# A two-block model on one core: the statistics, banks and order of the mLSTM mixer rearranged

## The chip, the core and the metric

The kernel runs on one core of a Trainium2 chip. A core has five engines that work side by side, each with its own queue of instructions: TensorE (PE, matmuls into the eight PSUM banks), VectorE (DVE), ScalarE (ACT, which loads a table for each family of functions), GpSimd (POOL) and SyncE (SP, which issues transfers here). They meet by semaphores alone. The metric is the device time of one execution in microseconds, the median of three runs.

## The reference, cut to what matters

The model is a hybrid block (a convolution branch and an mLSTM branch, then a mixture of experts) and a second block with a delta-rule mixer, attention and two feed-forward layers. Only the first block's mixer is touched:

```python
z = h @ w_in                       # 512 tokens, 1024 -> 5128 features
u = causal_dwconv(glu_a * sigmoid(glu_b), conv_dw_w, conv_dw_b)     # 31 taps
u = silu(layernorm(u, conv_ln_g, conv_ln_b))                        # over 512 channels
y_a = u @ w_conv_out                                                # 512 -> 1024
qk = silu(causal_dwconv(concat([q, k]), qk_conv_w, qk_conv_b))      # 4 taps
hm = mlstm_chunkwise(q, k, v, i_g, f_g)                             # 4 heads of 128
hm = (hm - mean) * rsqrt(var + eps) * m_norm_g * sigmoid(o)         # per head
y_b = hm @ w_m_out                                                  # 512 -> 1024
merged = sigmoid(g_a) * y_a + sigmoid(g_b) * y_b
x = x + gate * (merged @ w_out)
```

The kernel computes mLSTM in one piece per head: with running decay sums, weights exp(...) of every earlier token on every later one times the scores q.k give P; the numerator is v'P, the denominator the column sum of P, and h = numerator / max(|denominator|, exp(-m)).

## The kernel before

Features lie on the partitions, the 512 tokens along the free side. A is a big SBUF buffer of 59 rows of 512 columns; A[:, 8 to 11] hold the four heads' results, A[:, 40 to 43] the conv branch, A[:, 44 to 51] q and k, A[:, 16 to 19] v, A[:, 24 to 39] the two sets of gates, A[:, 52 to 55] a head's weights. PS is PSUM, eight banks of 128x512.

Projections are done in 40 tiles (p = 4g + j, ten groups of four), each of 24 matmuls: every product is made of three (high x high, high x low, low x high), for which ScalarE writes a weight piece's high part and VectorE its low part. Group g uses banks 4(g % 2) to 4(g % 2) + 3, and ScalarE copies every tile out, the last groups through a sigmoid. Behind them stands, in TensorE's order: the transposes of v for tokens (L607), the sums over channels for the conv norm's mean (L614) and variance (L618), four small transposes of gate values (L623), then the heads. ScalarE does Silu of q and k (L1203), the squares (L1207), the root by Ln and Exp (L1136, L1137) and Silu of the normed conv channels (L1212). Only then do the heads begin.

For each of four heads: TensorE spreads a row over the partitions (bank 4, L634), makes four score blocks in banks 0 to 3 (L640), and a second row (bank 5); VectorE copies the first row twice (L1733, L1734), ScalarE takes seven exponentials of it (L1237, L1240), VectorE multiplies scores and exponentials (L1759), TensorE makes numerators (bank 6, L650) and denominators (bank 7, L652), ScalarE takes the absolute value (L1242), VectorE the maximum, the reciprocal and the product (L1763 to L1765), which raises ml_h. TensorE waits for ml_h of a head before it starts the next head's numerators, and VectorE divides a head before it makes the next head's weights:

```python
for hd in range(MH):
    if hd:
        pe.wait_ge(S("ml_h"), hd)
    head_row(hd, 5, gr[7])
```

Between heads ScalarE and VectorE split one conv channel tile (L1244, L1767) and one out weight piece (L1220, L1741) into high and low parts. After head 3: means of all heads on TensorE (L659), differences (L1772), squares (L1248), sums (L662), Ln (L1251), Exp (L1254), and VectorE applies norm, gain and gate (L1775, L1776). TensorE waits for ml_std of all heads, then does 16 out tiles of 12 matmuls (q = 0 to 7 from conv_out, 8 to 15 from m_out), each multiplied by its gate on VectorE (L1786, L1792), summed in pairs (L1794), split (L1265, L1752), and eight w_out tiles of 24 matmuls, whose results are added to x (L1810). SyncE loads the second w_out unit when the last m_out tile is done, behind it x, and then the first experts' weights.

## Time and profile before

| | us |
|---|---|
| median of three runs (2561.7 to 2565.02) | 2563.48 |
| the profiled execution | 2564.16 |
| its span, first to last instruction | 2562.4 |
| TensorE busy in it | 2313.2 |
| VectorE busy | 1182.8 |
| ScalarE busy | 813.5 |
| mean granted TensorE clock, share of full | 0.942 |

Times in rows are microseconds from the span's start. The profile puts down what ended an engine's idle time, by semaphores; PE rows are pipelined, so starts tell more than lengths. The granted clock is 1.00 for 2.4 GHz and 0.50 for 1.2 GHz. Read a stage by what ends its idle times, not by the busy shares of the whole span.

### The profile page before, as it was taken

How to read it: one execution, taken by the hardware profiler on the slowest of the kernel's cores; microseconds unless marked ns; L12 is line 12 of the kernel's file. 1: busy time of each engine (PE TensorE's matmuls, PEld its weight loads, DVE VectorE, ACT ScalarE, POOL GpSimd, SP SyncE). 2: the span in 40 equal slices, each digit the busy share in tenths (PEclk: the TensorE clock that was granted, in tenths of full speed). 3: DMA queues.
4: the chain of work that ended last, by engine and by line, in shares of the span. 5: the costliest groups of instructions: out<-in, count | busy, mean ns of one | idle time of the engine just before them, and what ended most of it. 6: DMA issues, size and time to landing. Idle time of an engine off the chain costs nothing.

```text
span 2562.4 us, 29704 instructions
## 1 busy us (share of the span) xinstructions
PE 2313.2 (90%) x11748; PEld 1584.8 (62%) x11748; DVE 1182.8 (46%) x1716; ACT 813.5 (32%) x1251; POOL 119.6 (5%) x160
## 2 busy tenths in 40 slices
PE   6899878959999999957989498999999899999997
PEld 3688636623333333324768496888777787888775
DVE  3789345430000000025654743677843573677832
ACT  3222333321111111124455253323324283323322
POOL 0000000021111111100000200000000000000000
PEclk8999978979999999978989689999999999999999
DMA  8622200628999999830111001122222301222221
GB/s 356 226 79 92 92 0 33 277 91 332 375 378 399 386 389 385 359 137 34 66 66 66 1 34 66 66 98 98 99 99 99 132 1 66 81 90 95 95 99 66
DMA packets 36406, 384.56 MB, mean 150 GB/s; under 512 B 10080, under 2 KB 10336, under 8 KB 13408
## 3 DMA queue, kind: packets, MB, share of 16 engines
q1 hardware_dynamic: 27520, 374.91, 37.5%
q0 software_dynamic: 8800, 8.45, 1.0%
q8 instruction: 60, 0.98, 0.2%
q14 instruction: 26, 0.21, 0.0%
HBM read 384.10 MB, written 16.83 MB: 156 GB/s over the span
## 4 chain that ended last, share of the span: by engine, by line
PE 53%; DVE 16%; ACT 5%; issue 3%; DMA 1%; DVEq 1%; POOL 0%; ACTq 0%; SPq 0%; POOLq 0%
PE PS L744 9%; PE PS L570 9%; PE PS L571 9%; PE PS L572 8%; PE PS L783 4%; PE PS L764 4%; DVE ring_r L1946 3%; PE PS L791 2%; DVE A L1694 2%; ACT w_hi_r L1318 2%; PE PS L533 2%; DVE A L2156 1%; DVE sq L2154 1%; DVE A L2157 1%; DVE hid_r L2169 1%
## 5 line engine op out<-in xcount | busy, mean ns | idle before, releaser
L571 PE MATMUL PS<-h_r,w_hi_r 128*128 128x512 f32 x1104 | 432.5, 392 | 0.0
L570 PE MATMUL PS<-h_hi_r,w_hi_r 128*128 128x512 f32 x1056 | 418.0, 396 | 10.8 <-ACT A L1345 7.5
L572 PE MATMUL PS<-h_hi_r,ring_r 128*128 128x512 f32 x1056 | 413.3, 391 | 0.0
L1946 DVE TENSOR_TENSOR ring_r<-ring,w_hi_r 128x1024 fp32r<-128x1024 f32 x196 | 238.6, 1223 | 362.7 <-ACT w_hi_r L1318 362.7
L1318 ACT ACTIVATE w_hi_r<-ring 128x1024 fp32r<-128x1024 f32 x196 | 202.6, 1051 | 329.0 <-PE PS L572 203.9
L570 PEld LDWEIGHTS PS<-h_hi_r,w_hi_r 128*128 128x128 f32 x1056 | 199.7, 189 | 62.3 <-issue 17.2
L571 PEld LDWEIGHTS PS<-h_r,w_hi_r 128*128 128x128 f32 x1104 | 209.2, 190 | 45.0 <-issue 1.9
L572 PEld LDWEIGHTS PS<-h_hi_r,ring_r 128*128 128x128 f32 x1056 | 199.6, 189 | 42.1
L1922 DVE TENSOR_TENSOR A<-A,PS 128x512 f32<-128x512 f32 x16 | 11.0, 687 | 396.4 <-PE PS L744 396.4
L744 PE MATMUL PS<-A 128*64 128x512 f32 x768 | 170.4, 600 | 0.1
L570 PE MATMUL PS<-x_r,top_r 128*128 128x512 f32 x320 | 128.2, 400 | 12.0 <-DVE ring_r L1605 12.0
L571 PE MATMUL PS<-hid_r,w_hi_r 128*128 128x512 f32 x352 | 138.5, 393 | 0.0
L571 PE MATMUL PS<-h_r,top_r 128*128 128x512 f32 (+1 forms) x328 | 130.7, 398 | 0.0
L572 PE MATMUL PS<-x_r,ring_r 128*128 128x512 f32 x320 | 126.6, 395 | 0.0
L744 PEld LDWEIGHTS PS<-A 128*64 128x64 f32 x768 | 54.9, 138 | 113.2 <-issue 113.0
L783 PE MATMUL PS<-A 128*64 128x512 f32 x256 | 113.3, 595 | 0.0
L783 PE MATMUL PS<-h,A 128*64 128x512 f32 x256 | 113.3, 595 | 0.0
L764 PE MATMUL PS<-A 128*32 128x512 f32 x768 | 113.1, 594 | 0.0
L1694 DVE SCALAR_TENSOR_TENSOR A<-A,vec 128x511 f32<-128x511 f32 (+9 forms) x144 | 106.1, 737 | 4.1
L1497 ACT ACTIVATE A<-A 128x512 f32<-128x512 f32 x44 | 27.8, 632 | 250.7 <-DVE A L2157 250.7
L1170 ACT ACTIVATE top_r<-ring 128x1024 fp32r<-128x1024 f32 x40 | 42.4, 1060 | 168.7 <-PE PS L572 168.7
L570 PE MATMUL PS<-top_r,w_hi_r 128*128 128x512 f32 x208 | 83.0, 399 | 10.9 <-DVE ring_r L1946 6.7
(448 smaller groups left out, 3762.6 us busy)
## 6 DMA issues: line engine op xcount, KB each, us to landing
A<-wexp SPq DMA_DIRECT2D x64, 2048.0 KB, 12.3
ring<-wall SPq DMA_DIRECT2D x63, 2048.0 KB, 8.1
ring<-wexp SPq DMA_DIRECT2D x16, 2048.0 KB, 18.1
h<-wexp SPq DMA_DIRECT2D x16, 2048.0 KB, 13.2
A<-wada SPq DMA_DIRECT2D x12, 2048.0 KB, 14.7
x<-xt_in SPq DMA_DIRECT2D x2, 2048.0 KB, 12.1
A<-y_assignments SPq DMA_DIRECT2D x4, 1024.0 KB, 7.9
h_tokens<-A SPq DMA_DIRECT2D x4, 512.0 KB, 2.8
```

Source lines behind the costliest of these rows:

```text
L533: mm(PS[:, bank, :], ones, sq[:, k % 2, :], start=k == 0, stop=k == KD - 1).then_inc(S("sq_used"), 1)
L570: mm(out, w[0], x_[0], start=first, stop=False)
L571: mm(out, w[0], x_[1], start=False, stop=False)
L572: return mm(out, w[1], x_[0], start=False, stop=last_)
L744: last = mm(PS[HALF * j:HALF * (j + 1), bank, :], x_main[:, k // 4, (k % 4) * P + HALF * j:(k % 4) * P + HALF * (j + 1)], w[j][:, k, :], s ...
L764: last = mm(PS[r:r + QUARTER, 5, :], x_rest[:, k * HALF + QUARTER * j:k * HALF + QUARTER * (j + 1)], w[j][:, k, :], start=k == 0, stop=k = ...
L783: last = mm(PS[HALF * j:HALF * (j + 1), 6 + half, :], hT_main[:, k * P + HALF * j:k * P + HALF * (j + 1)], moe_dn[j][:, 4 * half + k, :], ...
L791: last = mm(PS[r:r + QUARTER, 5, :], hT_rest[:, k * HALF + QUARTER * j:k * HALF + QUARTER * (j + 1)], moe_dn[j][:, 4 * half + k, :], start ...
L1170: a_(in_hi(p), ring[:, g % 2, :, j * P:(j + 1) * P], ACT.Copy).then_inc(S("w_hi"), 1)
L1318: a_(w_hi_r[:, :, j * P:(j + 1) * P], ring[:, slot, :, j * P:(j + 1) * P], ACT.Copy).then_inc(S("w_hi"), 1)
L1694: ins = stt(dst[:, s:T], src[:, 0:T - s], w(j), dst[:, s:T], ALU.mult, ALU.add)
L1946: tt(ring_r[:, slot, :, cols], ring[:, slot, :, cols], w_hi_r[:, :, cols].bitcast(F32), ALU.subtract).then_inc(S("w_lo"), 1)
```

## The change

TensorE's order: the transposes of v go behind tile 36 (into banks 0 to 3), the conv mean and the small transposes behind tile 37, the conv variance (bank 3 in place of 2) behind tile 38. ScalarE copies v out after tile 36, and does the Silu of q and k and the conv squares after tile 37. Scores take three banks (the fourth block of 128 columns shares bank 1 with the second), numerators two in turn (6 and 3). A head's second row is made after the next head's scores, and waits for the division before. VectorE makes the next head's weights first and divides then; the conv channels are normed behind head 0's weights, their Silu lies behind head 0's exponentials on ScalarE. Conv pieces and inputs are split in sets (one, two, one input; one, one, two pieces) over heads 0 to 2. Out tiles 0 and 1 are before the head means, 2 and 3 before the head variances, 4 to 7 behind them, each in a bank of its own with a wait on one gate product in place of four; m_out and w_out tiles likewise. VectorE does gate products and pieces between the steps of the head norm. The short convolutions come in the order of the heads. In the diff, blank lines and parts that repeat the old text in another place are left out.

```diff
@@ -334,6 +334,30 @@
...
+        def mix_bank(q):
+            return 4 + q % 4 if q // 4 in (2, 4) else q % 4
+        def num_bank(hd):
+            return 6 if hd % 2 == 0 else 3
+        def s_row4(hd):
+            return 3 * hd if hd else 1
+        def s_scores(hd):
+            return 3 * hd + 1 if hd else 2
+        def s_row5(hd):
+            return 3 * hd + 5 if hd + 1 < MH else 3 * MH
+        HEAD_INPUTS, HEAD_PIECES = ((0,), (1, 2), (3,), ()), ((0,), (1,), (2, 3), ())
+        HEAD_ORDER = [hd + part for hd in range(MH) for part in (0, MH)]
+        def score_place(s):
+            return PS[:, (0, 1, 2, 1)[s], 384 * (s == 3):384 * (s == 3) + T - s * P]
@@ -580,6 +604,36 @@
...
+            def v_rows():
+                pe.wait_ge(S("ev_act"), 36)
+                for t in range(NT):
+                    for hd in range(MH):
+                        last = nc.tensor.transpose(PS[:, t, hd * P:(hd + 1) * P], A[:, 16 + hd, t * P:(t + 1) * P], ident)
+                last.then_inc(S("gT_mm"), 1)
+            def conv_mean():
+                pe.wait_ge(S("ev_act"), 38)
...
+                for i in range(CT):
+                    last = mm(PS[:, 0, :], ones, A[:, 40 + i, :], start=i == 0, stop=i == CT - 1)
...
+            def conv_var():
+                for i in range(CT):
+                    pe.wait_ge(S("cl_sq"), i + 1)
+                    last = mm(PS[:, 3, :], ones, A[:, 4 + i, :], start=i == 0, stop=i == CT - 1)
+                last.then_inc(S("cl_mm"), 1)
+            def gate_columns():
...
+                    last = nc.tensor.transpose(PS[:, 2, 256 + 4 * t:260 + 4 * t], gr[5][:, t * P:(t + 1) * P], ident[0:4, 0:4])
+                last.then_inc(S("gT_mm"), 1)
@@ -600,100 +654,99 @@
...
+                    if p == 36:
+                        v_rows()
+                    if p == 37:
+                        conv_mean()
+                        gate_columns()
+                    if p == 38:
+                        conv_var()
+            pe.wait_ge(S("g_rows"), 2)
+            pe.wait_ge(S("em"), 1)
             pe.wait_ge(S("gT_ev"), 1)
-            pe.wait_ge(S("cl_ev"), 1)
-            pe.wait_ge(S("em"), 1)
...
                 return mm(PS[:, bank, :], ident[0:4, hd:hd + 1].broadcast_to([4, P]), src, start=True, stop=True)
             def head_scores(hd):
+                pe.wait_ge(S("ev_act"), 39)
                 head_row(hd, 4, gr[6]).then_inc(S("ml_s"), 1)
+                pe.wait_ge(S("qk"), 2 * hd + 2)
                 for s in range(NT):
-                    last = mm(PS[:, s, 0:T - s * P], A[:, 48 + hd, s * P:(s + 1) * P], A[:, 44 + hd, s * P:T], start=True, stop=True)
+                    last = mm(score_place(s), A[:, 48 + hd, s * P:(s + 1) * P], A[:, 44 + hd, s * P:T], start=True, stop=True)
                 last.then_inc(S("ml_s"), 1)
+            def head_end(hd):
+                if hd:
+                    pe.wait_ge(S("ml_h"), hd)
+                head_row(hd, 5, gr[7]).then_inc(S("ml_s"), 1)
             head_scores(0)
+            pe.wait_ge(S("ev_act"), 41)
...
             for hd in range(MH):
                 if hd:
-                    pe.wait_ge(S("ml_h"), hd)
-                head_row(hd, 5, gr[7])
+                    pe.wait_ge(S("ml_ad"), hd)
                 for s in range(NT):
                     pe.wait_ge(S("ml_p"), NT * hd + s + 1)
-                    mm(PS[:, 6, s * P:T], A[:, 16 + s, hd * P:(hd + 1) * P], A[:, 52 + s, s * P:T], start=s == 0,
...
                 last.then_inc(S("ml_n"), 1)
                 if hd + 1 < MH:
                     head_scores(hd + 1)
...
+                head_end(hd)
+            def head_means():
+                pe.wait_ge(S("ml_h"), MH)
+                for hd in range(MH):
+                    mm(PS[:, 4 + hd, :], ones, A[:, 8 + hd, :], start=True, stop=True).then_inc(S("ml_mu"), 1)
+            def head_vars():
+                for hd in range(MH):
+                    pe.wait_ge(S("ml_sq"), hd + 1)
+                    mm(PS[:, 4 + hd, :], ones, A[:, 12 + hd, :], start=True, stop=True).then_inc(S("ml_var"), 1)
+            def out_tile_of(q, u_hi, u_lo):
...
+                pe.wait_ge(S("w_lo"), PIECES_IN + q + 1)
...
+                    last = product(PS[:, mix_bank(q), :], (out_hi(q)[:, k, :], w_lo[:, k, :]), (u_hi(k), u_lo(k)), k == 0, k == CT - 1)
+                last.then_inc(S("mm"), 1)
+            pe.wait_ge(S("h_lo"), KD + CT)
+            for q in range(8):
+                if q == 2:
+                    head_means()
+                if q == 4:
+                    head_vars()
+                if q >= 4:
+                    pe.wait_ge(S("ev_dve"), q - 3)
+                out_tile_of(q, lambda k: h_r[:, k, :], lambda k: h_hi_r[:, 2 + k, :])
             pe.wait_ge(S("ml_std"), MH)
...
+            pe.wait_ge(S("h_lo"), 2 * KD)
+            for q in range(8, 16):
+                if q >= 12:
+                    pe.wait_ge(S("ev_dve"), q - 7)
+                out_tile_of(q, lambda k: hid_r[:, 16 + k, :], lambda k: hid_r[:, 8 + k, :])
...
+            norm(1, NORM_BANK[1])
@@ -1187,29 +1240,27 @@
...
+                    if p == 36:
+                        act.wait_ge(S("gT_mm"), 1)
+                        a_(A[:, 16:20, :], PS[:, 0:4, :], ACT.Copy).then_inc(S("ev_act"), 1)
+                    if p == 37:
+                        for n, m in enumerate(HEAD_ORDER):
+                            act.wait_ge(S("qk_cv"), n + 1)
+                            a_(A[:, 44 + m, :], A[:, 44 + m, :], ACT.Silu).then_inc(S("qk"), 1)
+                        for i in range(CT):
+                            act.wait_ge(S("cl_d"), i + 1)
+                            a_(A[:, 4 + i, :], A[:, 40 + i, :], ACT.Square).then_inc(S("cl_sq"), 1)
...
+            inv_sqrt(rstd[:], PS[:, 3, :], 1, 1.0 / DC).then_inc(S("cl_ev"), 1)
@@ -1238,25 +1289,36 @@
...
+                if hd == 0:
+                    for i in range(CT):
+                        act.wait_ge(S("cl_n"), i + 1)
+                        a_(A[:, 40 + i, :], A[:, 40 + i, :], ACT.Silu, bias=V("conv_ln_b", i)).then_inc(S("ya_in"), 1)
                 act.wait_ge(S("ml_n"), hd + 1)
+                if hd:
+                    act.wait_ge(S("ml_h"), hd)
                 a_(A[:, 2, :], PS[:, 7, :], ACT.Abs).then_inc(S("ml_ad"), 1)
-                act.wait_ge(S("ya_in"), hd + 1)
-                a_(h_r[:, hd, :], A[:, 40 + hd, :], ACT.Copy).then_inc(S("h_hi"), 1)
-                out_w_hi(hd)
+                for i in HEAD_INPUTS[hd]:
+                    act.wait_ge(S("ya_in"), i + 1)
+                    a_(h_r[:, i, :], A[:, 40 + i, :], ACT.Copy).then_inc(S("h_hi"), 1)
+                for q in HEAD_PIECES[hd]:
+                    out_w_hi(q)
+            out_w_hi(4)
             for hd in range(MH):
                 act.wait_ge(S("ml_d"), hd + 1)
                 a_(A[:, 12 + hd, :], A[:, 8 + hd, :], ACT.Square).then_inc(S("ml_sq"), 1)
+            for q in range(5, 8):
+                out_w_hi(q)
             for hd in range(MH):
                 act.wait_ge(S("ml_var"), hd + 1)
                 last = a_(A[:, 4 + hd, :], PS[:, 4 + hd, :], ACT.Ln, bias=eps[:, 1:2], scale=1.0 / P)
...
+            for hd in range(MH):
+                out_w_hi(8 + hd)
+                act.wait_ge(S("hm"), hd + 1)
+                a_(hid_r[:, 16 + hd, :], A[:, 8 + hd, :], ACT.Copy).then_inc(S("h_hi"), 1)
+            for q in range(12, 16):
@@ -1709,7 +1771,7 @@
...
-            for m in range(8):
+            for m in HEAD_ORDER:
@@ -1720,16 +1782,19 @@
...
+            cp(gT[:], PS[:, 2, 256:272].rearrange("p (a b) -> p a b", b=MH)).then_inc(S("gT_ev"), 1)
+            def conv_normed():
+                dve.wait_ge(S("cl_ev"), 1)
+                dve.wait_ge(S("cl_d"), CT)
+                for i in range(CT):
+                    stt(A[:, 40 + i, :], A[:, 40 + i, :], V("conv_ln_g", i), rstd[:], ALU.mult, ALU.mult).then_inc(S("cl_n"), 1)
@@ -1751,45 +1816,71 @@
...
-            head_rows(0)
-            for hd in range(MH):
-                dve.wait_ge(S("ml_s"), 2 * hd + 2)
+            def head_weights(hd):
+                dve.wait_ge(S("ml_s"), s_scores(hd))
...
-                    stt(A[:, 52 + s, s * P:T], PS[:, s, 0:T - s * P], float(P) ** -0.5, A[:, 52 + s, s * P:T], ALU.mult, ALU.mult).then_inc(S("ml_p"), 1)
+                    stt(A[:, 52 + s, s * P:T], score_place(s), float(P) ** -0.5, A[:, 52 + s, s * P:T], ALU.mult, ALU.mult).then_inc(S("ml_p"), 1)
+            def head_divided(hd):
+                dve.wait_ge(S("ml_ad"), hd + 1)
+                dve.wait_ge(S("ml_s"), s_row5(hd))
+                link(tt(A[:, 2, :], A[:, 2, :], PS[:, 5, :], ALU.max))
+                link(nc.vector.reciprocal(A[:, 3, :], A[:, 2, :]))
+                tt(A[:, 8 + hd, :], PS[:, num_bank(hd), :], A[:, 3, :], ALU.mult).then_inc(S("ml_h"), 1)
+            head_rows(0)
+            head_weights(0)
+            conv_normed()
+            for hd in range(MH):
                 if hd + 1 < MH:
                     head_rows(hd + 1)
-                dve.wait_ge(S("ml_ad"), hd + 1)
-                link(tt(A[:, 2, :], A[:, 2, :], PS[:, 5, :], ALU.max))
-                link(nc.vector.reciprocal(A[:, 3, :], A[:, 2, :]))
-                tt(A[:, 8 + hd, :], PS[:, 6, :], A[:, 3, :], ALU.mult).then_inc(S("ml_h"), 1)
-                dve.wait_ge(S("h_hi"), KD + hd + 1)
-                tt(h_hi_r[:, 2 + hd, :], A[:, 40 + hd, :], h_r[:, hd, :].bitcast(F32), ALU.subtract).then_inc(S("h_lo"), 1)
-                out_w_lo(hd)
+                    head_weights(hd + 1)
+                head_divided(hd)
+                for i in HEAD_INPUTS[hd]:
+                    dve.wait_ge(S("h_hi"), KD + i + 1)
+                    tt(h_hi_r[:, 2 + i, :], A[:, 40 + i, :], h_r[:, i, :].bitcast(F32), ALU.subtract).then_inc(S("h_lo"), 1)
+                for q in HEAD_PIECES[hd]:
+                    out_w_lo(q)
...
+                dve.wait_ge(S("mm"), out_tile(q))
...
+                tt(u, u, PS[:, mix_bank(q), :], ALU.mult).then_inc(S("ev_dve"), 1)
...
+                dve.wait_ge(S("ml_std"), hd + 1)
+                link(stt(A[:, 8 + hd, :], A[:, 8 + hd, :], V("m_norm_g", hd), A[:, 4 + hd, :], ALU.mult, ALU.mult))
...
+            gated(0)
+            out_w_lo(4)
+            gated(1)
...
-                stt(A[:, 8 + hd, :], PS[:, hd, :], -1.0 / P, A[:, 8 + hd, :], ALU.mult, ALU.add).then_inc(S("ml_d"), 1)
+                stt(A[:, 8 + hd, :], PS[:, 4 + hd, :], -1.0 / P, A[:, 8 + hd, :], ALU.mult, ALU.add).then_inc(S("ml_d"), 1)
+            for q in (2, 3):
+                out_w_lo(q + 3)
+                gated(q)
+            out_w_lo(7)
...
+                head_normed(hd)
+                gated(4 + hd)
+                out_w_lo(8 + hd)
             for hd in range(MH):
-                out_w_lo(4 + hd)
                 dve.wait_ge(S("h_hi"), KD + CT + hd + 1)
                 tt(hid_r[:, 8 + hd, :], A[:, 8 + hd, :], hid_r[:, 16 + hd, :].bitcast(F32), ALU.subtract).then_inc(S("h_lo"), 1)
...
+                    q = 8 + 4 * m + j
+                    gated(q)
+                    if q < 12:
+                        out_w_lo(q + 4)
@@ -1805,7 +1896,7 @@
...
+                    src = PS[:, mix_bank(16 + k) if g in (G_WOUT, G_WOUT + 1) else 4 * (g % 2) + j, :]
...
-NORM_BANK = [0, 0, 0, 0, 4, 0, 4, 4]
+NORM_BANK = [0, 4, 0, 0, 4, 0, 4, 4]
```

## Rows read from the trace of the kernel before

**Rows 1.** Time line of TensorE: start, length, line, shapes, [idle before <-releaser].

```profile
305.61 1.97 PE L607 MATMUL PS<-cst,A 128*128 128x128 f32 x16 [0.69 <-ACT A L1192]
307.41 3.60 PE L614 MATMUL PS<-A,cst 128*128 128x512 f32 x8
...
315.64 6.57 PE L618 MATMUL PS<-A,cst 128*128 128x512 f32 x8 [4.63 <-ACT A L1207]
```

**Rows 2.** Time line of TensorE, start and third tile of w_out.

```profile
457.27 0.47 PE L570 MATMUL PS<-h_r,top_r 128*128 128x512 f32 x1 [2.16 <-issue]
...
470.72 0.50 PE L570 MATMUL PS<-h_r,top_r 128*128 128x512 f32 x1 [0.70 <-DVE ring_r L1747]
```

**Rows 3.** Time line of TensorE over heads 0 and 1.

```profile
335.93 1.12 PE L650 MATMUL PS<-A 128*128 128x512 f32 x2
...
340.44 1.12 PE L634 MATMUL PS<-A,cst 4*128 4x512 f32 x2
341.49 2.42 PE L640 MATMUL PS<-A 128*128 128x512 f32 x8
...
347.65 1.12 PE L634 MATMUL PS<-A,cst 4*128 4x512 f32 x2 [3.73 <-DVE A L1765]
...
349.45 2.08 PE L650 MATMUL PS<-A 128*128 128x512 f32 x2 [0.68 <-DVE A L1759]
...
356.99 1.12 PE L634 MATMUL PS<-A,cst 4*128 4x512 f32 x2
```

**Rows 4.** Time line of ScalarE behind the projections.

```profile
309.50 1.28 ACT L1203 ACT_TABLE_LOAD   x1
310.80 4.27 ACT L1203 ACTIVATE A<-A 128x512 f32<-128x512 f32 x8
...
322.25 0.69 ACT L1136 ACTIVATE rstd<-PS,eps 128x512 f32<-128x512 f32 x1 [3.80 <-PE PS L618]
```

**Rows 5.** Time line of TensorE from the last division to the first out tile.

```profile
393.81 6.74 PE L659 MATMUL PS<-A,cst 128*128 128x512 f32 x8 [5.52 <-DVE A L1765]
400.38 3.60 PE L662 MATMUL PS<-A,cst 128*128 128x512 f32 x8
...
409.27 0.77 PE L570 MATMUL PS<-h_r 128*128 128x512 f32 x1 [5.30 <-issue]
```

**Rows 6.** Stretches of time: us, busy (instructions) by engine, clock, DMA.

```profile
262.00:264.00 2.00, 2.00 (x10) 1.59 (x9) 1.93 (x4) 0.00 (x0) 0.00 (x0) 1.00 0.00 0
350.00:355.00 5.00, 5.00 (x8) 2.08 (x7) 0.39 (x2) 0.00 (x0) 0.00 (x0) 0.50 0.00 0
458.00:461.00 3.00, 3.00 (x8) 2.31 (x8) 2.93 (x6) 0.63 (x1) 0.00 (x0) 0.50 1.01 431
```

**Rows 7.** Time line of TensorE, the matmul behind a pause in the projections.

```profile
261.70 0.50 PE L570 MATMUL PS<-x_r,top_r 128*128 128x512 f32 x1 [1.77 <-DVE ring_r L1605]
```

**Rows 8.** Time line of VectorE, its wait for the residual input x.

```profile
469.44 1.23 DVE L1747 TENSOR_TENSOR ring_r<-ring,top_r 128x1024 fp32r<-128x1024 f32 x1 [6.08 <-DMA x<-xt_in]
```

**Rows 9.** Time line of ScalarE, one of the pieces that wait for an out tile.

```profile
428.01 0.63 ACT L1220 ACTIVATE h_r<-ring 128x512 fp32r<-128x512 f32 x1 [2.09 <-PE PS L572]
```

**Rows 10.** Time line of ScalarE, first and last of head 1's seven exponentials.

```profile
342.92 0.40 ACT L1237 ACTIVATE A<-A,gT 128x128 f32<-128x128 f32 x1 [0.74 <-DVE A L1734]
...
345.01 0.38 ACT L1237 ACTIVATE A<-A,gT 128x128 f32<-128x128 f32 x1
```

**Rows 11.** Time line of VectorE, division of head 0.

```profile
341.60 0.69 DVE L1733 COPY A<-PS 128x512 f32<-128x512 f32 x1 [5.11 <-PE PS L634]
...
342.81 0.68 DVE L1763 TENSOR_TENSOR A<-A,PS 128x512 f32<-128x512 f32 x1
...
346.90 0.69 DVE L1765 TENSOR_TENSOR A<-PS,A 128x512 f32<-128x512 f32 x1
347.51 0.68 DVE L1767 TENSOR_TENSOR h_hi_r<-A,h_r 128x512 fp32r<-128x512 f32 x1
```

**Rows 12.** Time line of VectorE, the norm of head 0 applied.

```profile
407.65 0.75 DVE L1775 SCALAR_TENSOR_TENSOR A<-A,vec 128x512 f32<-128x512 f32 x1 [6.38 <-ACT A L1254]
```

118 lines of the change are left out of this document (25 added, 93 removed).

## Prediction

> **What bounds the kernel now.** I read the chain of waits first: its share-of-span line is TensorE above all, so a change of the mixer counts only where TensorE stands still or runs slowly. The stretches of time with the granted clock come next, because this part of the kernel is the one with many low ones, then the time lines of TensorE, ScalarE and VectorE from 305 to 475 us. The reader is to see four things there.
>
> First, the projections end at 305.61 - 0.69 = 304.92 [rows 1], and the last m_out tile at 457.27 - 2.16 = 455.11 [rows 2]. All that the change moves lies in these 150.2 us. Second, between the projections and the first numerator at 335.93 [rows 3] TensorE has only transposes, two column sums and the first scores; it waits 4.63 us for ScalarE's squares and then for the root [rows 1, 4]. Third, a head is a ring: numerators, scores of the next head, 3.73 us of waiting until VectorE has divided, then 0.68 us for the next weights [rows 3]. Last, behind the last division come sums, Ln, Exp and the norm, with 5.30 us of idle TensorE before the first out tile at 409.27 [rows 5]. After such waits the clock is low, 1.2 GHz: 0.50 in 350 to 355, and 0.50 in 458 to 461 after 2.16 us of idling; a pause of 1.77 us before 261.70 left it at 1.00 in 262 to 264 [rows 2, 6, 7]. Numerators take 340.44 - 335.93 = 4.5 us at full clock and 356.99 - 349.45 = 7.5 us at the low one [rows 3].
>
> **Behind m_out nothing gets nearer.** SyncE issues the second w_out unit and x when m_out is done; VectorE stands 6.08 us for x and goes on at 469.44, 14.3 us after m_out's end [rows 8], and the third w_out tile starts 15.6 us after it [rows 2]. This offset stays. So the gain is the shift of m_out's end, less what happens to the clock before that third tile. The expert loads, too, are released by m_out's end or later and move along.
>
> **A. Statistics and transposes between tiles 36 and 39.** TensorE does 16 transposes (307.41 - 305.61 = 1.8), two groups of eight passes (3.6 each; today's second took 6.57 at low clock, between fast tiles I take 3.6, as the first has [rows 1]) and the four small transposes (a quarter of the sixteen, 0.45): 9.5 us. Tile 39 ends at 304.9 + 9.5 = 314.4. ScalarE's eight Silu and four squares (4.27 for eight, so 6.4, and a table load of 1.28 [rows 4]) lie beside tile 38: tile 37 ends at 304.9 less two tiles of 5.44 (twice 2.72 [rows 9]) plus 1.8, 295.9; with the last weight piece and the eviction behind it (1.6) the Silu start at 297.5 and the squares end near 305.2. Tile 38, behind the means, ends at 305.3. That cover has no slack; each us more there would be a us of stall. VectorE's short convolutions, only put in another order, end before tile 36 does and cost nothing.
>
> **B. Up to the first numerator.** ScalarE takes tile 39 out (0.6, as [rows 9]), then table load and Ln (1.28 + 0.69 [rows 4]) and the same for Exp: 318.9. Head 0's exponentials follow in that table; the seven take 345.39 - 342.92 = 2.5 us [rows 10], the first two 0.8 and a product 0.6 (my reading of the pipeline). Numerators start at 320.4 where today it is 335.9. TensorE idles from 314.4 + 1.05 + 2.4 (head row and scores [rows 3]) = 317.9 to there, 2.5 us.
>
> **C. The heads.** With the division behind the next head's weights, the numerators of a head no longer wait for it. The ring is now VectorE's: row copies 1.2 to 1.3 [rows 11], exponentials with the last product 2.8 [rows 10], division 347.59 - 342.81 = 4.8, and two, three and three small splits of 0.6 each [rows 11]. In head 0, ScalarE adds the Silu of the four conv channels and two table loads, so head 1's exponentials start at 329.1 (numerators end 324.9, Silu 326.2, three short copies 327.8, load 1.3). Then: products 331.9, division 336.7, splits 337.9, rows 339.2; products 342.0, division 346.8, splits 348.6, rows 349.9; products 352.7, division 357.5. The last head row (1.1) ends at 358.6, three splits at 359.3, the last division at 364.1. The period is 10.1 and 10.7 us; TensorE's own work per head is 4.5 + 1.05 + 2.4 + 1.05 = 9.0. So it idles 1.1 to 1.7 us per head instead of 3.73 + 0.68. The two numerator banks, the new waits on the row and on ml_ad are met before this ring in every head: numerator bank 3 or 6 was read one division earlier. Behind the wait of ScalarE's Abs for the division before stand only its copies and the next exponentials, which wait for VectorE's rows anyhow.
>
> **D. Out tiles around the head norms.** A tile takes 0.63 + 2.09 = 2.72 us [rows 9]. Conv tiles 0 and 1 run from 358.6 beside the last division to 364.1, means 3.6 (second row of [rows 5]) to 367.7, tiles 2 and 3 to 373.1, squares' sums 3.6 to 376.7, tiles 4 to 7 to 387.6. Beside these run the table load and four Ln (377.9), load and four Exp (381.5). VectorE then needs 1.4 for a head's norm (0.75 [rows 12] and a product of 0.65), 0.6 for the gate of a tile and 0.6 for a weight piece: from the first piece at 382.7 three times 2.6, then four splits of 0.6, gives 392.9. TensorE has idled 5.3 us by then, as long as today. Eight m_out tiles, 21.8, end at 414.7.
>
> **E. Clock.** That sum is at full clock. Today 3.73 us of idling cost head 1's numerators 3.0, and 2.16 us cost 3 us at half speed, 1.5 [rows 2, 3, 6]. These are my bounds for one fall. Two waits are that long after the change, B's 2.5 and D's 5.3; I take 1.7 for each, nearer to the short one because the work behind is dense: m_out ends at 418.1, 37.0 us before today's end. The waits of 1.1 to 1.7 in the heads I count at nothing: TensorE has about a us of room there, and the pause of 1.77 us left the clock up; at worst they cost 3.0 less 1.0 per head.
>
> **F. Before the third w_out tile.** Two tiles need 10.9; started 0.5 us after m_out and held about 1.5 by the last sums' splits, they end 12.9 after it, against 470.02 - 455.11 = 14.9 today [rows 2]. The wait for x grows from 0.70 to 2.7 us and lets the clock fall once more: 1.7 (bounds 0 and 3.0).
>
> **Sum.** -37.0 + 1.7 = -35.3, rounded -35. The profiled execution lasted 2564.16 us (span 2562.4) and the median is 2563.48, so 0.7 less than it: 2529 for an execution like the profiled one, 2528.5 for the median.
>
> **A page against the sum.** ScalarE changes tables eight times here where it did seven times (a Sigmoid load for tile 38 is new, two around head 0 change place). In the rows a change costs the load alone: 309.50 + 1.28 = 310.78, and the next instruction starts at 310.80 [rows 4]. The Trainium skill, "ScalarE: Activation LUTs", section "What ACT_TABLE_LOAD costs", gives about 1283 ns for the load, which agrees, and about 1380 ns of draining besides, which these rows do not show. If the one more change carried that drain, the sum would be 1.4 us smaller, -34.
>
> **The rivals.** (1) *The clock falls in the heads too.* For: TensorE has a short wait in every head, beside the small row matmuls. Against: the 1.77 us pause [rows 7]. Price: 2.0 in each of four heads, 8 us: 2536.5. (2) *Conv tiles hide nothing.* If weight pieces or gates came late, the path from the last division would be as long as today, 455.11 - 393.81 = 61.3 [rows 2, 5]: 364.1 + 61.3 = 425.4, plus B's 1.7 and F's 1.7, gives -26: 2537.5. Against: gate, piece and difference together are under 2.5 us per tile of 2.72. (3) *No fall costs anything*, because the low stretches lie where TensorE waits anyhow: 414.7 against 455.1, -40: 2523.5. (4) *Slower: TensorE stays at 1.2 GHz.* Heads (36), norms (7.2) and 16 tiles (43.5) are 87 us at 2.4 GHz; all at the low level they end at 314.4 + 174 + some 5 of waits = 493, 38 us late: 2601. It decides when about 46% of this work (40 of 87 us) runs low; today the low share is large only because the waits are 3.7 to 5.5 us long. The Trainium skill, "TensorE: Matmul & The Clock Gate", section "A second HAM failure mode: psum-queue depth-cycling", says that short idles between groups of matmuls that cycle through banks can make the clock oscillate; by that rule rival 1 or 4 would come true, while the trace has both a pause that did it and one that did not. That the change does not do what it says is rival 2.
>
> **Chances.** Forecast 0.74, rival 1 0.12, rival 2 0.05, rival 3 0.07, rival 4 0.02. The range, 2521 to 2537, takes in rivals 1 and 3 with the bounds of E and F. A difference under 0.2% (5 us) is about what a measurement of this kernel cannot tell from none. Slower holds rival 4, 0.02; the same 0.01; faster 0.97.
>
> **What would show it.** A: tile 39 ends near 314.4, no wait of TensorE for squares above 1 us. B: first numerator near 320.4. C: divisions end 10.1 to 10.7 apart. D: out tile 0 starts before the last division ends, an idle of about 5 us before tile 8. E: clock 1.00 in most of 325 to 387. F: third w_out tile 15.6 us after m_out's end, after a wait near 2.7. I am wrong by most if that offset does not hold, if ScalarE becomes the heads' ring through its table loads, or if the low clock covers several heads.

## The result, and the profile after

| | before | after |
|---|---|---|
| median, us | 2562.59 (2555.64 to 2565.02) | 2521.67 (2519.7 to 2523.14) |
| span of the profiled execution | 2562.4 | 2521.3 |
| TensorE busy | 2313.2 | 2296.5 |
| VectorE / ScalarE busy | 1182.8 / 813.5 | 1182.7 / 814.4 |
| mean granted clock | 0.942 | 0.950 |

The ratio is 0.9848, with a 95% interval of 0.9835 to 0.9861: 41 us less, where 35 were forecast. TensorE does the same 11748 instructions with 16.7 us less busy time; that difference is clock. The rest is time in which it no longer stands.

The time lines are of one execution. The time line of TensorE in the kernel after (start, duration, engine, line, operation, in brackets the idle time ahead and what ended it). L695 are numerators, L670 a head's row, L707 and L713 the head means and variances, L594 the first matmul of a tile.

```profile
309.91 1.12 PE L670 MATMUL PS<-A,cst 4*128 4x512 f32 x2
...
316.29 1.10 PE L695 MATMUL PS<-A 128*128 128x512 f32 x2 [2.91 <-DVE A L1824]
...
325.68 1.10 PE L695 MATMUL PS<-A 128*128 128x512 f32 x2 [0.38 <-DVE A L1824]
...
335.65 1.10 PE L695 MATMUL PS<-A 128*128 128x512 f32 x2 [0.96 <-DVE A L1824]
...
346.22 1.10 PE L695 MATMUL PS<-A 128*128 128x512 f32 x2 [1.57 <-DVE A L1824]
...
351.98 1.12 PE L670 MATMUL PS<-A,cst 4*128 4x512 f32 x2 [1.20 <-DVE A L1832]
353.02 0.50 PE L594 MATMUL PS<-h_r 128*128 128x512 f32 x1
...
358.62 3.59 PE L707 MATMUL PS<-A,cst 128*128 128x512 f32 x8
...
367.54 3.60 PE L713 MATMUL PS<-A,cst 128*128 128x512 f32 x8
...
387.19 0.76 PE L594 MATMUL PS<-hid_r,h_r 128*128 128x512 f32 x1 [5.14 <-issue]
...
412.36 0.47 PE L594 MATMUL PS<-h_r,top_r 128*128 128x512 f32 x1 [0.39 <-issue]
...
427.35 0.76 PE L594 MATMUL PS<-h_r,top_r 128*128 128x512 f32 x1 [2.33 <-DVE ring_r L1812]
```

These rows answer [rows 1, 2, 3, 5]. Tile 39 ends at 309.9, where the head row starts. The 3.73 us of waiting per head are 0.38, 0.96 and 1.57. Out tile 0 starts at 353.02; the last division ends only at 358.43. The last m_out tile ends at 412.36 - 0.39 = 411.97, before at 455.11.

The same kernel on ScalarE (Silu of q and k, squares, the conv channels' Silu, head 1's exponentials) and on VectorE (conv norm, last division, low part of the third w_out tile), which answer [rows 4, 8, 10, 11]:

```profile
294.58 4.28 ACT L1255 ACTIVATE A<-A 128x512 f32<-128x512 f32 x8
298.76 2.18 ACT L1258 ACTIVATE A<-A 128x512 f32<-128x512 f32 x4
...
316.94 1.28 ACT L1295 ACT_TABLE_LOAD   x1
318.23 2.56 ACT L1295 ACTIVATE A<-A,vec 128x512 f32<-128x512 f32 x4
...
322.53 1.28 ACT L1288 ACT_TABLE_LOAD   x1
323.83 0.40 ACT L1288 ACTIVATE A<-A,gT 128x128 f32<-128x128 f32 x1
```

```profile
317.20 2.73 DVE L1793 SCALAR_TENSOR_TENSOR A<-A,vec,rstd 128x512 f32<-128x512 f32 x4
...
357.74 0.69 DVE L1832 TENSOR_TENSOR A<-PS,A 128x512 f32<-128x512 f32 x1
...
425.98 1.22 DVE L1812 TENSOR_TENSOR ring_r<-ring,top_r 128x1024 fp32r<-128x1024 f32 x1 [7.53 <-DMA x<-xt_in]
```

And stretches of time of the kernel after, against [rows 6] (bounds, length, busy time of PE, PEld, DVE, ACT, POOL, then the granted clock, DMA share and GB/s):

```profile
320.00:330.00 10.00, 9.62 (x34) 5.38 (x32) 6.38 (x8) 6.18 (x13) 0.00 (x0) 1.00 0.00 0
387.00:391.00 4.00, 3.81 (x9) 3.07 (x10) 0.08 (x1) 0.00 (x0) 0.00 (x0) 0.50 0.47 197
428.00:431.00 3.00, 3.00 (x9) 2.36 (x8) 1.65 (x2) 0.00 (x0) 0.00 (x0) 0.56 1.00 426
```

The clock is full in the heads and at its low level twice: behind the 5.14 us ahead of m_out, and behind the 2.33 us in w_out.

**How executions are compared below.** Two stretches that these versions do not change scatter between executions. The end of head 0's scores (first numerators less their idle) lies at 313.35 to 318.62 us in eleven profiles with the order of after, and from the experts' first product to the end pass 2004.0 to 2007.5 us in all fourteen profiles. So I give, beside the medians, the *inner stretch* between these two landmarks; it is 514.23 - (316.29 - 2.91) = 200.85 us in the kernel after.

### The profile page after: what moved, and what is told of

The parts are those of the page before. It is cut to its first block, busy times and chain, and to the rows that moved or that the text cites. A ratio compares the mean times of both kernels' runs of the same rounds, so it can differ in the third digit from the quotient of the medians.

```text
span 2521.3 us, 29727 instructions
## 1 busy us (share of the span) xinstructions
PE 2296.5 (91%) x11748; PEld 1577.7 (63%) x11748; DVE 1182.7 (47%) x1716; ACT 814.4 (32%) x1252; POOL 119.5 (5%) x160
## 4 chain that ended last, share of the span: by engine, by line
PE 46%; DVE 21%; ACT 6%; issue 5%; DVEq 1%; DMA 1%; POOL 0%; ACTq 0%; SPq 0%; POOLq 0%
PE PS L797 9%; PE PS L594 6%; PE PS L595 6%; PE PS L596 6%; PE PS L836 4%; PE PS L817 4%; DVE ring_r L2037 4%; ACT w_hi_r L1380 3%; DVE A L2247 2%; PE PS L844 2%; DVE A L1756 2%; DVE sq L2245 2%; DVE A L2248 2%; DVE A L2246 2%; PE PS L557 2%
## 5 line engine op out<-in xcount | busy, mean ns | idle before, releaser
L594 PE MATMUL PS<-h_hi_r,w_hi_r 128*128 128x512 f32 x1056 | 418.2, 396 | 10.8 <-ACT A L1407 7.4
L594 PEld LDWEIGHTS PS<-h_hi_r,w_hi_r 128*128 128x128 f32 x1056 | 199.7, 189 | 62.2 <-issue 17.3
L594 PE MATMUL PS<-x_r,top_r 128*128 128x512 f32 x320 | 128.6, 402 | 9.7 <-DVE ring_r L1667 9.7
L594 PE MATMUL PS<-top_r,w_hi_r 128*128 128x512 f32 x208 | 83.0, 399 | 11.0 <-DVE ring_r L2037 6.7
```

The costliest lines, as they stand in the source:

```text
L594: mm(out, w[0], x_[0], start=first, stop=False)
```

## Experiments

Each edit is against the kernel after, except for the second.

**1. VectorE divides first again.** VectorE makes a head's division and splits ahead of the next head's weights.

```diff
             for hd in range(MH):
-                if hd + 1 < MH:
-                    head_rows(hd + 1)
-                    head_weights(hd + 1)
                 head_divided(hd)
                 ...splits of the head...
+                if hd + 1 < MH:
+                    head_rows(hd + 1)
+                    head_weights(hd + 1)
```

> The changed kernel with VectorE's order in the heads put back: rows of the next head, division, splits, and only then the next head's weights. Theory of the chain: the next numerators then start about 11.3 us after the end of the last ones (head row 1.0, scores 2.4 and second row 1.0, division 4.8, splits 1.2 to 1.8, first product 0.6) where they start 5.4 to 6.1 us after it now; the divisions end about 16 us apart, three times 5.5 us are lost, 16 us, and 1.5 to 3 us more for each head in which the clock falls in the longer wait: 2538 to 2547. Rival (what the change gave here is the clock, not the order): the divisions stay near 10 to 11 us apart and the time within 5 us of 2521.7.

Measured: 2546.25 us (2542.83 to 2548.83), ratio 0.9935 (0.9921 to 0.9948) to before, 24.6 more than after. TensorE, numerators of the four heads:

```profile
318.60 1.10 PE L695 MATMUL PS<-A 128*128 128x512 f32 x2 [2.91 <-DVE A L1824]
...
336.16 2.04 PE L695 MATMUL PS<-A 128*128 128x512 f32 x2 [6.86 <-DVE A L1824]
...
354.59 2.04 PE L695 MATMUL PS<-A 128*128 128x512 f32 x2 [7.46 <-DVE A L1824]
...
374.03 2.04 PE L695 MATMUL PS<-A 128*128 128x512 f32 x2 [7.46 <-DVE A L1824]
```

Heads are 17.6 to 19.4 us apart, not 10, and the numerators behind each wait take 2.04 instead of 1.10. The time lies in the forecast range. The order of the division is the largest single part.

**2. Before, with its waits filled.** The old kernel with 4, 6, 5 (heads 1 to 3), 7 and 5 sums that nobody reads, put ahead of its waits (one of the places shown).

```diff
+            for _ in range(7):
+                mm(PS[:, 3, P:T], ones, A[:, 32, P:T], start=True, stop=True)
             pe.wait_ge(S("ml_h"), MH)
```

> The kernel before, with TensorE's waits of 3.7 to 5.6 us filled by column sums that nobody reads (4 and 6 of 512 columns ahead of the heads, 5 of 384 behind each head's scores, 7 of 384 ahead of the head means, 5 of 512 ahead of the first out tile), each filling a little shorter than its wait at full clock. No result and no wait is changed. Theory of the clock: the low stretches between 315 and 413 us go, which cost 19 us in the profile (variance sums 3.0, head 0's rows and scores 3.2, numerators 7.2 and a row 0.9, means 3.0, first out tile 2.0): 2544 to 2549, with TensorE's own work in the stage at its short durations. Theory that the waits alone matter: 0 to 5 us slower than before, 2563 to 2568.

Measured: 2546.7 us (2541.7 to 2547.0), ratio 0.9933 (0.9919 to 0.9947), 15.7 less than before, with more work. Its stretches, and those of before beneath:

```profile
310.00:325.00 15.00, 13.54 (x37) 5.75 (x35) 4.42 (x10) 12.08 (x18) 0.00 (x0) 1.00 0.00 0
325.00:335.00 10.00, 8.94 (x24) 4.50 (x23) 2.05 (x5) 4.38 (x11) 0.00 (x0) 0.83 0.00 1
360.00:440.00 80.00, 74.69 (x282) 51.77 (x282) 49.99 (x70) 30.70 (x51) 0.00 (x0) 1.00 0.09 31
```

```profile
310.00:325.00 15.00, 7.92 (x15) 3.03 (x13) 2.75 (x7) 11.12 (x18) 0.00 (x0) 0.77 0.11 44
325.00:335.00 10.00, 6.84 (x11) 3.33 (x12) 4.28 (x8) 7.12 (x13) 0.00 (x0) 0.50 0.00 1
360.00:440.00 80.00, 61.04 (x193) 39.27 (x192) 42.45 (x57) 25.79 (x47) 0.00 (x0) 0.85 0.07 26
```

No semaphore wait was removed, and over a third of the 41 us came back, as forecast (2544 to 2549). The waits of before cost twice: their own length, and some 16 us of slow work behind them.

**3. Statistics behind tile 39.** The transposes of v, the conv mean, variance and small transposes go behind the last projection tile again, and with them ScalarE's copy of v, Silu of q and k and squares. The norm and Silu of the conv channels stay in head 0.

```diff
-                    if p == 36:
-                        v_rows()
-                    if p == 37:
-                        conv_mean()
-                        gate_columns()
-                    if p == 38:
-                        conv_var()
+            v_rows()
+            conv_mean()
+            conv_var()
+            gate_columns()
```

> The changed kernel with the value transposes, the conv sums and the small transposes (and ScalarE's copy, Silu and squares) behind tile 39 again; the Silu and the norm of the conv channels stay in head 0. Theory of the chain: from tile 36's end to the first numerator 31.9 us now; then the ScalarE chain behind the value transposes (copy 1.9, table 1.3, twelve functions 6.4), sums 3.6 or 6.6 at low clock, Ln and Exp with tables 3.9, exponentials and product 1.6 follow tile 39 directly: 7 us more at full clock, 8.5 to 10 with a fall: 2529 to 2532. Rival (the 15.5 us of this stage all come from moving the sums): 15 us or more, 2537.

Measured: 2532.3 us (2529.96 to 2532.49), ratio 0.9879 (0.9864 to 0.9894), 10.6 more than after. TensorE waits 1.97 us ahead of the means, 2.40 ahead of the variances, and then for the transposed gates and the weights:

```profile
306.97 3.27 PE L620 MATMUL PS<-A,cst 128*128 128x512 f32 x7 [1.97 <-ACT A L1250]
...
313.07 5.33 PE L627 MATMUL PS<-A,cst 128*128 128x512 f32 x8 [2.40 <-ACT A L1256]
...
319.27 1.09 PE L667 MATMUL PS<-A,cst 4*128 4x512 f32 x2 [0.54 <-DVE gT L1781]
```

The cover of A is real, and the variances (5.33 against 3.6) ran partly at the low clock. The rival, that all of this stage's gain comes from moving these steps, would have cost 15 us or more. From 335.93 to 320.5 (316.29 + 4.2, see below) the first numerators had come 15.4 us nearer, so some 5 us are left for what this edit does not undo, the conv norm and Silu in head 0, and for the low clock in that stretch of before. No run takes these apart.

**4. All out tiles behind the head norm.** TensorE's means and variances ahead of tile 0, ScalarE's pieces and VectorE's gates behind the norm.

```diff
+            head_means()
+            head_vars()
+            pe.wait_ge(S("ml_std"), MH)
             pe.wait_ge(S("h_lo"), KD + CT)
             for q in range(8):
-                if q == 2:
-                    head_means()
-                if q == 4:
-                    head_vars()
...
+            for q in range(8):
+                gated(q)
+                out_w_lo(8 + q)
```

> The changed kernel with no out tile ahead of the head norm: head means, head sums of squares and the wait for all four roots first, then the 16 out tiles, and VectorE's and ScalarE's steps in the old order; banks and the waits on single tiles stay. Theory of the chain: from the last division's end to m_out's end 61.4 us before, 53.5 now; so 8 us more (5.5 us of tiles beside the last division, and the waits of 5.3 and 1.0 us that tiles 2 to 7 cover partly), 2529 to 2531. Rival (the interleaving hides nothing, since an equally long wait of 5.1 us stands ahead of tile 8 now): 2 us or less, 2522 to 2524.

Measured: 2544.25 us (2541.53 to 2545.49), ratio 0.9933 (0.9920 to 0.9946), 22.6 more than after, where 8 were expected: a miss by a factor of two to three. I took the surplus for the shared banks and tried the same with the banks of before.

**5. The same with the banks of before.**

```diff
         def mix_bank(q):
-            return 4 + q % 4 if q // 4 in (2, 4) else q % 4
+            return 4 * (q // 4 % 2) + q % 4
```

> The kernel with the output tiles behind the head norm lost 22.6 us to the changed kernel where 8 to 10 were forecast. In its trace conv_out tiles 5 to 8 each wait 2.10 us for the gate of the tile four places back, which VectorE reaches only after the tile before has ended, because the changed kernel keeps conv_out tiles 0 to 3 and 4 to 7 in the same four banks. This kernel is that one with the banks of before (tiles 4 to 7 in banks 4 to 7). Theory (the surplus is the shared banks, an artefact of undoing the order without the banks): those waits (2.71 + 4 x 2.1 = 11.1 us) and the lower clock beside them (some 2 to 3 us) go, so 2531 (2529 to 2534). Rival (the tiles in the changed kernel hide far more than 8 us of statistics): it stays at 2540 to 2546.

Measured: 2544.03 us (2540.12 to 2551.68), as before this edit and in the rival's range. TensorE:

```profile
358.46 5.74 PE L707 MATMUL PS<-A,cst 128*128 128x512 f32 x8 [5.39 <-DVE A L1828]
364.04 3.60 PE L713 MATMUL PS<-A,cst 128*128 128x512 f32 x8
372.88 0.79 PE L594 MATMUL PS<-h_r 128*128 128x512 f32 x1 [5.24 <-ACT A L1312]
...
388.32 0.50 PE L594 MATMUL PS<-h_r 128*128 128x512 f32 x1 [2.70 <-DVE A L1848]
393.46 0.80 PE L594 MATMUL PS<-h_r 128*128 128x512 f32 x1 [2.10 <-DVE A L1848]
...
400.09 0.78 PE L594 MATMUL PS<-h_r 128*128 128x512 f32 x1 [2.10 <-DVE A L1848]
...
406.81 0.68 PE L594 MATMUL PS<-h_r 128*128 128x512 f32 x1 [2.10 <-DVE A L1848]
...
435.37 0.47 PE L594 MATMUL PS<-h_r,top_r 128*128 128x512 f32 x1 [2.17 <-issue]
```

The banks had moved, but I had left TensorE's wait for the gate four tiles back (`ev_dve`, q - 3) in the loop. It did not say which bank was meant: VectorE reaches that gate behind a piece whose high part ScalarE writes only after the tile before. So both kernels measure my own wait too, and the number of the fourth experiment is no price of D; nor does the rival follow from it. The trace still bounds the price, by a count of this one execution. Numerators start at 316.26 here and 316.29 in after, and the heads are equal up to 351.95. m_out ends at 433.20, 21.2 later. Of this 2.70 + 3 x 2.10 = 9.0 is the wait I put in; 5.39 + 5.24 - 5.14 = 5.5 is what D had hidden; the remaining 6.7 is lower clock, which belongs to both. By this count D's order is worth 5.5 to 12.2 us. A kernel with that wait removed as well was not run, and whether another wait would then take its place is not shown.

**6. The fall ahead of m_out.** Five sums that nobody reads, ahead of tile 8.

```diff
             pe.wait_ge(S("ml_std"), MH)
+            for _ in range(5):
+                mm(PS[:, 4, :], ones, A[:, 12, :], start=True, stop=True)
```

> The changed kernel with five column sums of 512 that nobody reads in the 5.1 us wait ahead of tile 8 (4.5 us at full clock). The wait's end does not move. If the wait lets the clock fall, the eight m_out tiles get their 2.7 us back: 2519. If the clock falls for another reason, or the fillers delay tile 8, nothing or a us is lost: 2521.7 to 2522.7.

Measured: 2521.42 us (2515.43 to 2523.25), no difference in the medians, where 2519 was expected.

```profile
388.38 4.45 PE L735 MATMUL PS<-A,cst 128*128 128x512 f32 x10
393.64 0.50 PE L594 MATMUL PS<-hid_r,h_r 128*128 128x512 f32 x1 [0.80 <-DVE hid_r L1879]
```

The clock in 380 to 395 is 1.00 where it was 0.77, so the idle does cause the fall. The eight m_out tiles take 415.70 - 393.64 = 22.1 us against 411.97 - 387.19 = 24.8: the 2.7 of the forecast came. It does not show further out, because the clock of this execution fell in places where the profile of after has no fall. In the heads that cost 1.7. In out tiles 0 and 1 (clock 0.82 and 0.83 in 355 to 365, 1.00 in after) it cost 1.5: tile 8 starts 36.7 us behind the last head row and not 35.2. The fillers are not to blame for that, since the third experiment, which has none, shows 36.8. A gain of 2.7 is below what the medians of these few runs can tell.

**7. The head variances early.** They stand directly behind the means, ahead of tile 2 and not of tile 4. ScalarE's and VectorE's steps of the norm come earlier among the pieces and gates to match (not shown):

```diff
                 if q == 2:
                     head_means()
-                if q == 4:
                     head_vars()
```

> The changed kernel with the head sums of squares right behind the head means (ahead of tiles 2 and 3), and VectorE's norms and splits for m_out ahead of the gates and pieces of tiles 4 to 7. The roots come 4.6 us earlier and the splits are ready before tile 7 ends, by the chain: the 5.1 us wait ahead of tile 8 goes and the low clock behind it (2.7), 0.9 us of waiting for squares comes: 6 to 7 us, 2515. If VectorE is the bound in this stretch (its 20 us of norms, gates and pieces), the wait stays at 3 us or more and the gain is under 3 us.

Measured: 2514.42 us (2512.36 to 2519.66), ratio 0.9822 (0.9806 to 0.9837), 7.3 less than after. The 5.14 us ahead of tile 8 and the fall behind it are gone; tile 8 has no idle of its own, and the next is w_out's:

```profile
410.93 0.47 PE L594 MATMUL PS<-h_r,top_r 128*128 128x512 f32 x1 [0.39 <-issue]
```

```profile
387.00:391.00 4.00, 4.00 (x19) 3.26 (x18) 4.00 (x8) 0.63 (x1) 0.00 (x0) 1.00 0.44 90
```

From the last head row to m_out's end: 410.54 - 357.12 = 53.4 us, 6.6 less than the 411.97 - 351.98 = 60.0 of after. The 5.14 and the 3.0 of low clock make 8.1; this execution has the fall in out tiles 0 and 1 too (0.85 and 0.80 in 355 to 365), which takes 1.5 back.

**8. x loaded early.** SyncE issues x behind unit 11 in its queue, not behind the second w_out unit:

```diff
+                if u == 11:
+                    sp.dma_start(x[:], xt_in).then_inc(S("x_in"), 16)
...
-            sp.wait_ge(S("mm"), UNIT_USED["in9"])
-            sp.dma_start(x[:], xt_in).then_inc(S("x_in"), 16)
```

> The changed kernel with the load of x issued when the projections are done, instead of behind the second w_out unit. If x holds the third w_out tile: its wait of 2.3 us goes, and with it the low clock behind it (1.5): 4 us, 2517.7, the third tile starts where the second ends. If the weight piece or the pieces' order holds it, nothing is gained: 2521.7 within 1 us.

Measured: 2517.28 us (2515.3 to 2518.7), ratio 0.9820 (0.9806 to 0.9833), 4.4 less. TensorE has no wait left ahead of the third w_out tile, and VectorE waits for ScalarE there, not for x:

```profile
421.10 1.23 DVE L1810 TENSOR_TENSOR ring_r<-ring,top_r 128x1024 fp32r<-128x1024 f32 x1 [2.35 <-ACT top_r L1277]
```

So F's offset was x, as the prediction read it, and its price is the 2.33 us and a fall: from m_out's end to the experts' first product pass 97.6 us here (509.89 - 412.27) and 102.3 in after (514.23 - 411.97), 4.6 less.

**9. x and variances early together.** Both edits above.

> The changed kernel with x loaded early (alone -4.4 us) and the head variances after conv_out tile 8's place taken by their own (alone -7.3 us), without the three high parts taken early by ScalarE. Theory (the two gains add, since they lie in different stages; from first numerators to the experts' first product the traces lose 5.9 and 6.1 us): 2510 to 2511.5, and the version with all three edits (2512.8) was no faster for its third. Rival (the gains overlap): 2513 to 2515.

Measured: 2512.11 us (2510.04 to 2517.98), 9.6 less than after, ratio 0.9805 (0.9791 to 0.9819) to before. The inner stretch is 191.53, 9.3 shorter, where the two alone made it 5.9 and 4.5 shorter. The median lies between the two forecasts and 2.1 short of the sum of the single gains, and settles nothing. The stages do: from the first numerators to m_out's end pass 90.8 us here and in the seventh experiment, 95.7 in after; from there to the experts' first product 97.8 here and 97.6 in the eighth. They add.

**10. All three.** With three high parts of the merged sums written by ScalarE between the m_out pieces as well:

```diff
             for q in range(8, 16):
                 out_w_hi(q)
+                if q >= 13:
+                    act.wait_ge(S("merged"), q - 12)
+                    a_(merged_hi(q - 13), A[:, 11 + q, :], ACT.Copy).then_inc(S("h_hi"), 1)
```

> e7 and the early load of x together, and the first three high parts of the merged sums put on ScalarE between the last out pieces instead of behind them. Each by the chain: 6.5 + 4.4, and up to 2.1 of the time by which the first two w_out tiles exceed 10.9 us: 13 us less than the changed kernel, 2508 to 2511. If the gains overlap (VectorE catching up later), less than 9 us.

Measured: 2512.83 us (2510.28 to 2515.78), 8.8 less than after: short of the forecast of 2508 to 2511, and by the number in the rival's "less than 9", though the ninth shows that the gains do not overlap. Its inner stretch is 190.09; the third edit is worth 1.4 there (it takes the waits of 0.39 and 1.18 in w_out) and nothing that the medians show.

**11. The fall ahead of the numerators.** Four sums that nobody reads, in the kernel after.

```diff
             pe.wait_ge(S("cl_ev"), 1)
+            for _ in range(4):
+                mm(PS[:, 6, :], ones, A[:, 32, :], start=True, stop=True)
             for hd in range(MH):
```

> The changed kernel with four sums that nobody reads ahead of head 0's first numerators, where TensorE idles 2.91 us. Theory (step B as forecast: that idle lets the clock fall to half, and it costs 1.7 us; one profile of five shows no fall, the others do): 1.2 to 1.7 us faster than the changed kernel, 2519.5 to 2520.5, and all head stages from 320 to 345 us at clock 1.00. Rival (the fall is made up for by waits further on): 2521.5 as the changed kernel.

Measured: 2525.7 us (2524.95 to 2527.08), 4 more than after, where up to 1.7 less was expected.

```profile
315.49 3.67 PE L691 MATMUL PS<-A,cst 128*128 128x512 f32 x8 [1.31 <-ACT rstd L1192]
319.00 1.02 PE L697 MATMUL PS<-A 128*128 128x512 f32 x2
```

I had placed the sums behind a wait for the conv norm's root, which ends 1.31 us into the idle. Then 3.67 us of sums fill the 1.6 that are left, and numerators start 4.82 us behind the scores instead of 2.91. The inner stretch is 3.2 longer: 1.9 are that delay, and 1.6 a fall in out tiles 0 and 1 (last head row to tile 8 in 36.8 us, not 35.2), so the heads were not all at 1.00 either (0.90 and 0.76 in 335 to 345). Since after shows no fall ahead of the numerators in its profile, nothing here tests what filling that idle would give.

**12. All three, and the same four sums.**

> The version with x early, variances early and three high parts interleaved (2512.8), with the same four unread sums ahead of head 0's first numerators. Theory (the fall after the 2.91 us idle costs 1.7 us in most executions): 2510.5 to 2511.5. Rival (made up for later): 2512.8.

Measured: 2514.19 us (2509.53 to 2515.68), ratio 0.9811 against 0.9817 for the tenth: no difference that can be told, and neither theory's number. The inner stretch is 188.22, 1.9 shorter, and the clock is 1.00 in 320 to 330, so in this execution the sums may have paid in spite of the delay. By the medians they are not worth having.

## Why the prediction was right, step by step

The forecast was 2528.5 in 2521 to 2537; the time is 2521.7, only 0.7 us inside the range's lower end, and that it lies inside is in part luck. The mechanism held. The size was off by 6 of 41 us, and the steps say where, for this pair of executions. The profile of after runs ahead already in unchanged code: ScalarE writes tile 36's first high part at 284.53, before at 288.70, 4.2 later. Of these, 2.7 are there at the pause of [rows 7] (259.00 against 261.70) and at the wait ahead of it (251.54 against 254.24); where they come from I did not trace. The other 1.5 are clock. In before, the next wait for a weight piece took 3.02 us and the clock behind it was 0.57 (270 to 274). In after the clock had fallen ahead of that wait (0.65 in 262 to 264), where the wait took it up: it was 1.42 us, at 267.79, with full clock behind it. I add 4.2 to after's times to compare.

- **A** held: tile 39 ends at 309.9 + 4.2 = 314.1 (314.4 forecast). ScalarE's Silu and squares took 4.28 + 2.18 beside tile 38, no wait for them is in the rows.
- **B** held in place, not in clock: the first numerator at 316.29 + 4.2 = 320.5 (320.4), idle 2.91 (2.5). The clock stayed full in this profile, so the 1.7 of E for B was not lost. Over executions it was sized right: from first numerators to the last head row pass 351.98 - 316.29 = 35.69 us in after and 35.69 in the fifth experiment, but 37.38 in the fourth, sixth, seventh, ninth and tenth, all with the same 2.91 us of idle. The fall costs 1.69.
- **C** held: divisions end 9.97, 10.58 and 6.51 us apart (10.1, 10.7, 6.6). They end 1.1 to 1.5 us earlier than forecast. The Silu table is loaded at 316.94, before its first input is made (317.20 on VectorE), and head 1's exponentials start at 328.0, not 329.1; that this is the whole reason is argued, not tested. The waits of 0.38 to 1.57 left the clock at 1.00 in this execution and cost nothing, as the prediction counted them. That is not so in all of them (see below).
- **D** held: tile 0 before the last division's end, idle 5.14 (5.3), m_out from 391.4 (392.9).
- **E**, the fall in m_out, was mis-sized for this execution: eight tiles take 411.97 - 387.19 = 24.8 us and 21.8 at full clock, so 3.0, my upper bound, not 1.7. I had priced it by the 2.16 us wait of [rows 2]; this idle is 5.14, and the one of 3.73 in [rows 3] cost 3.0. But neither row settles it: the same tiles behind the same 5.14 or 5.15 us took 24.7 us in experiments 3 and 11, and 23.5 and 23.4 in experiments 1 and 8. So the fall costs 1.6 to 3.0, which is close to the bounds that the prediction gave, 1.5 and 3.0.
- **F** held: third w_out tile 427.35 - 411.97 = 15.4 us behind m_out (15.6), wait 2.33 (2.7). The experts start 41.4 us earlier where m_out ended 43.1 earlier: 1.7 lost, as put down.

For this pair the sum for m_out's end is then -37.0 forecast, -4.2 upstream, -1.7 no fall in B, -1.5 the earlier chain, +1.3 the dearer fall in D: -43.1. **What failed is the reference point**: the sum was set against one execution of before, which ran late in untouched projections. Experiment 2, whose code up to there is that of before, ends its projections at 301.45, not 304.92. So about 3.5 of the 6 us can be the scatter of one profile. The time itself is 6.8 us under the forecast; the last 0.9 is that the median of before came out at 2562.59, not 2563.48. Whether the change itself also makes falls up there rarer stays open: eleven traces of the new order span 5.3 us at that point, and of the old there are two.

**Rival 1 came true in part.** The clock did fall behind short waits within the heads in seven of the other profiles (experiments 3, 4, 6, 7, 9, 10 and 11), each time in head 2's numerators behind 0.96 us of idle. In six of these (all but the fourth, which has no tiles there) it fell once more in out tiles 0 and 1, behind the 1.1 us ahead of the last head row. This is the third experiment:

```profile
323.63 1.10 PE L692 MATMUL PS<-A 128*128 128x512 f32 x2 [0.91 <-DVE A L1819]
...
342.99 1.36 PE L692 MATMUL PS<-A 128*128 128x512 f32 x2 [0.96 <-DVE A L1819]
...
359.32 1.12 PE L667 MATMUL PS<-A,cst 4*128 4x512 f32 x2 [1.11 <-DVE A L1827]
...
396.11 0.77 PE L594 MATMUL PS<-hid_r,h_r 128*128 128x512 f32 x1 [5.15 <-issue]
```

```profile
342.00:347.00 5.00, 4.04 (x7) 1.81 (x7) 4.79 (x6) 1.62 (x6) 0.00 (x0) 0.67 0.00 0
359.50:364.50 5.00, 5.00 (x13) 3.39 (x13) 4.96 (x5) 0.45 (x1) 0.00 (x0) 0.66 0.00 0
```

The fall in head 2 costs nothing: the last head row comes 359.32 - 323.63 = 35.69 us behind the first numerators, as in after. The room of about a us per head that the prediction counted on is real. The fall in out tiles 0 and 1 costs 1.6: 396.11 - 359.32 = 36.8 us to tile 8 against 387.19 - 351.98 = 35.2. No term of the prediction has it. So rival 1's price of 8 us is out, but an execution can lose 1.6 us here that the profile of after does not show.

Rival 3, that no fall costs anything, gave 2523.5, which is nearer to the time than the forecast, but for another reason: the falls in m_out and w_out did cost 3.0 and 1.7. Rival 2 would have shown m_out's end 61.3 us behind the last division; it is 53.5. Rival 4, 2601, is out.

**The page.** The forecast set the drain of "ScalarE: Activation LUTs" in the Trainium skill, section "What ACT_TABLE_LOAD costs", against the rows. The load at 322.53 takes 1.28 and the next instruction starts at 323.83, so again no drain, and the sum without it was the right one. The Trainium skill, "TensorE: Matmul & The Clock Gate", section "A second HAM failure mode: psum-queue depth-cycling", would have the clock oscillate in heads with short idles through banks. In the profile of after it does not (1.00 in all stretches of 5 us from 310 to 385). In seven others it falls and recovers between short idles, as above, which agrees with the section; the times of rivals 1 and 4 do not follow all the same, since the engine waits anyhow behind most of these falls. In experiment 8 the numerators at 347.76 took 2.05 behind 1.57 us of idle, and m_out started 71.1 us behind the first numerators against 70.9: 0.2 us.

**The parts.** Undone one at a time they cost 24.6 (division), 10.6 (statistics) and 5.5 to 12.2 (out tiles): 41 to 47 against the 41 of all. Some of it is counted twice, since each wait that comes back also brings a fall. The score and numerator banks and the conv norm in head 0 have no experiment of their own. The faster versions, the ninth and the tenth, leave no idle above 0.4 us between the last head row and w_out.

## What to carry to other kernels

Find the engine whose one long instruction (here a reciprocal of 3.35 us) stands between two uses of a faster engine, and let it do what the others wait for first; that reorder alone was 25 of 41 us. Price every wait that goes with the slow work behind it, as a range and not as one number (the same 5.14 us cost 1.6 to 3.0 here), and take the forecast's zero from more than one execution if the clock has fallen in untouched code. Compare stretches between two landmarks when an edit is worth less than the scatter of the whole. When you undo an order for an experiment, undo its semaphores too: a wait that was free in one order bound every tile in the other.
